# Seven block products in place of eight for the gate and up tiles of a feed-forward layer

## The chip, the cores and the metric

The kernel runs on one core of one Trainium2 chip. The metric is the device time of one execution in microseconds, as the median of several runs. One execution is profiled as well, and its trace is what the rows below come from. TensorE (PE) multiplies, VectorE (DVE) and ScalarE (ACT) do the elementwise work, GpSimd (POOL) helps a little, and SyncE (SP) issues the DMAs that bring the weights in.

## What is computed

The reference is a model of two layers over 544 tokens (512 of a prompt and 32 of a decoding batch), with a model width of 1024. Each layer has a mixer (stick-breaking attention in the first, an RWKV-7 time mix in the second), a cross-attention to a memory, and a feed-forward block. Only the last is touched:

```python
def rms_norm(x, gain):
    xf = x.astype(jnp.float32)
    y = xf * lax.rsqrt(jnp.mean(xf * xf, axis=-1, keepdims=True) + NORM_EPS)
    return (y * gain.astype(jnp.float32)).astype(x.dtype)

def swiglu_ffn(h, w_gate_up, w_down):
    gate, up = jnp.split(h @ w_gate_up, 2, axis=-1)
    return (jax.nn.silu(gate) * up) @ w_down
...
        h = rms_norm(x, p['norm_ffn'][layer])
        x = x + swiglu_ffn(h, p['ffn_w_gate_up'][layer], p['ffn_w_down'][layer])
```

The hidden width is 2816, which is 22 tiles of 128 rows. Everything is float32.

## The kernel before

Activations stand with the model's width on the partitions, so a matrix of weights is cut into units of 1024 x 128, each landing as eight 128 x 128 blocks in one of four slots of `weight_ring`. A float32 product is made of three passes of a faster type (fp32r): every operand is split into a high part, which is the value rounded to that type, and a low part, which is the rest, and PE adds high x high, high x low and low x high in PSUM. The 544 tokens are cut into two halves of 272 (`HALF`), one PSUM bank each. A unit is therefore 8 blocks x 3 passes x 2 halves = 48 matmuls of 128 x 272 (`multiply_unit`, line 235, the matmul on line 259), each with a weight load of its own.

`feed_forward` (line 1945) is one stage with a program for each engine, and it runs once a layer. PE first multiplies the 8 units of the cross-attention's output projection (`o`), then the 44 units of `up` (22 tiles, for each a gate unit and an up unit), then the 24 units of `down`. The up units after the first four run in a loop of 10 passes with two tiles each.

- **DVE** splits each unit in place (`split_unit`, line 277): `take_high` (line 205) writes the high part to one of two buffers, `take_low` (line 210) leaves the low part in the ring. It empties PSUM: `gate` (line 1961) multiplies the gate by the norm's factor, and `multiply` (line 1966) does the same to the up half, multiplies the two, and splits the hidden tile at once into the high and low parts that `down` reads.
- **ACT** does little in this stage: SiLU on each gate tile (line 2045). In the loop a load of its function table stands ahead of every two tiles.
- **SP** loads a unit into a slot as soon as PE is done with the unit in it (`stream_weights`, line 218).

Every engine runs its own instructions strictly in the order written; semaphores tie them together. `down` may start its first unit when 8 hidden tiles have been split, its second with 15, its third with all 22 (`down.ready`). Stages end with a barrier (line 179), and when a stage leaves more than `SEMS_KEPT` semaphores in use they are cleared, with one more barrier (line 173).

Of the kernel before, what the change touches and what calls it, by code (L numbers as in the profile page):

```python
# [23 lines left out]
P = 128  # L24
# [24 lines left out]
SEMS_KEPT = 60  # L49
# [74 lines left out]
class Core:  # L124


    def __init__(self, nc, ctx, ins, outs):
# [5 lines left out]
        self.high, self.high_r = self.aliased("weights_high", [P, 2, UNIT_KT, P])  # L133
        self.psum = ctx.enter_context(nc.psum_tensor("psum", [P, 8, 512], F32))
# [1809 lines left out]

def feed_forward(c, name, o, up, down, nxt, norm, tail, hidden, gated, out, low_rank=None):
# [6 lines left out]
    for job in (up, down) + ((nxt,) if nxt else ()):  # L1952
        job.begin(c)
    silu_taken, multiplied, high, low, scaled = (c.sem(name + x) for x in (
        "_silu_taken", "_multiplied", "_hidden_high", "_hidden_low", "_scaled"))
    down.ready = {0: (low, 8), 1: (low, 15), 2: (low, FT)}
# [4 lines left out]
    def gate(it, i):  # L1961
        nc.vector.wait_ge(*done(c, up, 2 * i, it))
# [3 lines left out]
    def multiply(it, i):  # L1966
        full, tile_high, tile_low = (t[:, bass.ds(it * 2 + i, 1), :] for t in (hidden.full, hidden.high, hidden.low))
        nc.vector.wait_ge(*done(c, up, 2 * i + 1, it))
        nc.vector.tensor_tensor(halves(full), c.psum[:, 4 * i + 2:4 * i + 4, 0:HALF], norm.inverse(),
                                ALU.mult).then_inc(c.slot_emptied[2 * i + 1], 1)  # L1970
        nc.vector.wait_ge(*out_of(c, up, 2 * i + 1, it))
        nc.vector.wait_ge(silu_taken, it * 2 + (i + 1))
        nc.vector.tensor_tensor(full, full, gated[:, i:i + 1, :], ALU.mult).then_inc(multiplied, 1)  # L1973
        nc.vector.wait_ge(multiplied, it * 2 + (i + 1))
        take_high(c, tile_high, full).then_inc(high, 1)
        nc.vector.wait_ge(high, it * 2 + (i + 1))
        take_low(c, tile_low, full, tile_high).then_inc(low, 1)
# [3 lines left out]
    with c.stage() as block:  # L1981
        @block.sync
        def _(sp):
            stream_weights(c, sp, o, up)
            stream_weights(c, sp, up, down)
            if low_rank:
                low_rank.load(sp)
            stream_weights(c, sp, down, nxt)
            if not nxt:
                tail.store(sp, halved)  # L1990

        @block.tensor
        def _(pe):
# [12 lines left out]
            with pe.Fori(1, up.iters) as it:  # L2006
                for u in range(RING):
                    multiply_unit(c, pe, up, it, u)
            if nxt:
                with pe.Fori(0, down.iters) as it:  # L2010
                    for u in range(down.per):
                        multiply_unit(c, pe, down, it, u)
# [7 lines left out]
            else:  # L2020
                for u in range(down.per):
                    multiply_unit(c, pe, down, 0, u)
                    if u >= 3 and u % 3 == 0:
                        tail.turn(pe, u // 3 - 1)
# [11 lines left out]
        @block.scalar  # L2036
        def _(act):
            for k in range(KT):
                norm.scalar(act, k)
            nc.scalar.preload_act_table_set("natural_log_exp_and_others")  # L2040
            norm.take_root(act)
            with act.Fori(0, up.iters) as it:
                for i in range(2):
                    act.wait_ge(*out_of(c, up, 2 * i, it))
                    nc.scalar.activation(gated[:, i, :], gated[:, i, :], ACT.Silu).then_inc(silu_taken, 1)  # L2045
            nc.scalar.preload_act_table_set("natural_log_exp_and_others")
            for k in range(KT):
                tail.scalar(act, k)
                if not nxt and k < KT - 1:
                    tail.keep(act, k)  # L2050
            tail.take_root(act)
            if not nxt:
                tail.divide_by_scalar(act, halved)

        @block.vector
        def _(dve):
# [8 lines left out]
            norm.take_low(dve, KT - 1)  # L2065
            split_unit(c, dve, up, 0, 2)
            dve.wait_ge(norm.inverted, 1)
            gate(0, 0)
            split_unit(c, dve, up, 0, 3)
            multiply(0, 0)  # L2070
            with dve.Fori(1, up.iters) as it:
                split_unit(c, dve, up, it, 0)
                gate(it - 1, 1)
                split_unit(c, dve, up, it, 1)
                multiply(it - 1, 1)
                split_unit(c, dve, up, it, 2)
                gate(it, 0)
                split_unit(c, dve, up, it, 3)
                multiply(it, 0)
            split_unit(c, dve, down, 0, 0)  # L2080
            gate(up.iters - 1, 1)
            split_unit(c, dve, down, 0, 1)
            multiply(up.iters - 1, 1)
            for n in range(down.n):
# [4 lines left out]
                if n + AHEAD < down.n:  # L2089
                    split_unit(c, dve, down, (n + AHEAD) // down.per, (n + AHEAD) % down.per)  # L2090
            if nxt:
# [1251 lines left out]
def build(nc, ins, outs):  # L3343
    with ExitStack() as ctx:
# [27 lines left out]
        def up_job(layer):  # L3372
            w = ins["ffn_w_gate_up"][layer].rearrange("(k p) m -> p k m", p=P)
            return Job(2 * FT, KT, lambda it, u: w[:, :, bass.ds(it * (2 * P) + (u // 2) * P + (u % 2) * FF, P)],
# [124 lines left out]
```

## Time and profile before

| | |
|---|---|
| median of 3 runs | 2107.98 us (2106.9 to 2118.1) |
| the profiled execution | 2109.09 us, of it the span of its instructions 2107.4 us |
| mean granted TensorE clock | 0.986 |
| busy: PE, weight loads, DVE, ACT, POOL | 2007.5, 1886.0, 1144.0, 544.6, 205.2 us |
| instructions | 46663, of them 20636 matmuls |

The two stages of the change stand at about 522 to 983 us (layer 1, counted from one) and at about 1642 to 2107 us (layer 2). A busy share is a mean over stages that have different limits, so it is read by stage. The profile models the end of a matmul, so that matmuls that stream back to back overlap: the spacing of their starts is the rate, the duration is the latency of one.

### The profile page before, as it was taken

How to read it: one execution, taken by the hardware profiler on the slowest of the kernel's cores; microseconds unless marked ns; L12 is line 12 of the kernel's file. 1: busy time of each engine (PE TensorE's matmuls, PEld its weight loads, DVE VectorE, ACT ScalarE, POOL GpSimd, SP SyncE). 2: the span in 40 equal slices, each digit the busy share in tenths (PEclk: the TensorE clock that was granted, in tenths of full speed). 3: DMA queues.
4: the chain of work that ended last, by engine and by line, in shares of the span. 5: the costliest groups of instructions: out<-in, count | busy, mean ns of one | idle time of the engine just before them, and what ended most of it. 6: DMA issues, size and time to landing. Idle time of an engine off the chain costs nothing. (4 is left out here: it accounts for less than half of the span.)

```text
span 2107.4 us, 46663 instructions
## 1 busy us (share of the span) xinstructions
PE 2007.5 (95%) x20636; PEld 1886.0 (89%) x20636; DVE 1144.0 (54%) x1578; ACT 544.6 (26%) x1012; POOL 205.2 (10%) x291
## 2 busy tenths in 40 slices
PE   8998999998999999999999878879999999999998
PEld 7997779996999999997988867668998899999997
DVE  5336886454656555336557734337654565555433
ACT  2005874113210110001237433334212211010111
POOL 5000001000200000110000345410010100000000
PEclk9999999999999999999999999999999999999999
DMA  4234212351323323332222000023351232333222
GB/s 133 82 123 143 61 32 81 121 164 57 90 81 90 90 85 101 95 85 57 70 71 61 8 4 4 4 72 102 103 168 41 61 90 81 88 90 88 83 83 79
DMA packets 299361, 169.77 MB, mean 81 GB/s; under 512 B 10328, under 2 KB 294176, under 8 KB 299200
## 3 DMA queue, kind: packets, MB, share of 16 engines
q1 hardware_dynamic: 294976, 151.25, 25.0%
q10 hardware_dynamic: 4224, 16.12, 2.0%
q8 instruction: 132, 2.16, 0.4%
q14 instruction: 29, 0.24, 0.0%
HBM read 155.94 MB, written 11.41 MB: 79 GB/s over the span
## 5 line engine op out<-in xcount | busy, mean ns | idle before, releaser
L259 PE MATMUL psum<-words_r,weights_high_r 128*128 128x272 f32 (+1 forms) x7808 | 1320.0, 290 | 7.4 <-PEq L179 3.7
L259 PEld LDWEIGHTS psum<-words_r,weights_high_r 128*128 128x128 f32 x7808 | 1117.0, 189 | 19.4 <-issue 15.1
L259 PE MATMUL psum<-words_r,weight_ring_r 128*128 128x272 f32 (+1 forms) x3904 | 829.3, 289 | 0.0
L259 PEld LDWEIGHTS psum<-words_r,weight_ring_r 128*128 128x128 f32 x3904 | 620.2, 190 | 0.0
L205 DVE TENSOR_SCALAR weights_high_r<-weight_ring 128x1024 fp32r<-128x1024 f32 (+1 forms) x258 | 177.9, 690 | 517.2 <-PE psum L259 513.2
L210 DVE TENSOR_TENSOR weight_ring_r<-weight_ring,weights_high_r 128x1024 fp32r<-128x1024 f32 (+1 forms) x264 | 319.4, 1210 | 11.2 <-ACT weights_high_r L350 2.3
L2045 ACT ACTIVATE words<-words 128x544 f32<-128x544 f32 x44 | 29.1, 660 | 448.3 <-DVE words L1963 448.3
L405 POOL TENSOR_TENSOR words<-words,words 128x544 f32<-128x544 f32 x35 | 61.6, 1760 | 766.0 <-ACT words L392 766.0
L2806 PE MATMUL psum<-words 64*64 64x64 f32 (+1 forms) x3168 | 90.8, 236 | 20.7 <-issue 17.5
L2806 PEld LDWEIGHTS psum<-words 64*64 64x64 f32 x3168 | 71.4, 135 | 34.9 <-issue 31.5
L210 DVE TENSOR_TENSOR words_r<-words,words_r 128x544 fp32r<-128x544 f32 (+5 forms) x124 | 87.7, 720 | 7.9 <-ACT words_r L337 2.6
L382 DVE TENSOR_TENSOR words<-psum,words 128x544 f32<-128x544 f32 x40 | 29.0, 725 | 108.1 <-PE psum L259 108.1
L389 ACT ACTIVATE words_r<-words,vector_columns 128x544 fp32r<-128x544 f32 x32 | 24.0, 751 | 154.9 <-DVE words L382 154.9
L392 ACT ACTIVATE words<-words 128x544 f32<-128x544 f32 x40 | 25.8, 646 | 129.9 <-DVE words L382 129.9
L397 DVE SCALAR_TENSOR_TENSOR words_r<-words,vector_columns,words_r 128x544 fp32r<-128x544 f32 x32 | 55.5, 1745 | 0.0
L2680 DVE TENSOR_TENSOR words<-psum,words 128x256 f32<-128x256 f32 x54 | 20.6, 419 | 58.7 <-PE psum L2806 58.7
L1831 POOL TENSOR_TENSOR words<-words,words 128x544 f32<-128x544 f32 x6 | 8.8, 1467 | 375.8 <-ACT words L1817 375.8
L1185 DVE SCALAR_TENSOR_TENSOR words<-psum,words 128x512 f32<-128x512 f32 (+2 forms) x40 | 32.5, 812 | 13.4 <-ACT words L1257 13.0
L928 ACT COPY words<-psum 128x512 f32<-128x512 f32 x16 | 9.4, 588 | 112.0 <-PE psum L867 112.0
L1174 DVE TENSOR_SCALAR words<-psum 128x512 f32<-128x512 f32 (+2 forms) x40 | 32.1, 806 | 5.4 <-PE psum L1057 2.7
L1585 PE MATMUL psum<-words,words 128*128 128x256 f32 x128 | 31.8, 408 | 3.2 <-PEq L179 3.2
L1973 DVE TENSOR_TENSOR words<-words,words 128x544 f32 (+1 forms) x44 | 32.0, 726 | 5.0
(346 smaller groups left out, 1947.7 us busy)
## 6 DMA issues: line engine op xcount, KB each, us to landing
weight_ring<-in_ffn_w_gate_up_dram SPq DMA_DIRECT2D x88, 512.0 KB, 3.9
weight_ring<-in_xa_w_kv_dram SPq DMA_DIRECT2D x32, 512.0 KB, 3.9
weight_ring<-in_ffn_w_down_dram SPq DMA_DIRECT2D x32, 448.0 KB, 3.6
weight_ring<-in_sb_w_qkv_dram SPq DMA_DIRECT2D x24, 512.0 KB, 3.8
weight_ring<-in_xa_w_q_dram SPq DMA_DIRECT2D x16, 512.0 KB, 4.0
weight_ring<-in_xa_w_o_dram SPq DMA_DIRECT2D x16, 512.0 KB, 3.8
weight_ring<-in_ffn_w_down_dram SPq DMA_DIRECT2D x16, 512.0 KB, 3.9
weight_ring<-in_sb_w_o_dram SPq DMA_DIRECT2D x8, 512.0 KB, 3.9
```

The source lines that it names most:

```text
L205: return c.nc.vector.tensor_scalar(high, full, 1.0, None, ALU.mult)
L210: return c.nc.vector.tensor_tensor(low, full, high.bitcast(F32), ALU.subtract)
L259: last = nc.tensor.matmul(c.psum[0:job.m(u), job.bank(q) + h, 0:w], weights[:, k, :], x[:, k, h * w:(h + 1) * w], start=job.opens(u) and k ...
L382: self.c.nc.vector.tensor_tensor(out, psum_of(self.c, self.job, u), out, ALU.add).then_inc(self.c.slot_emptied[self.job.slot(u)], 1)
L397: self.c.nc.vector.scalar_tensor_tensor(out=self.low_part[:, k, :], in0=self.x[:, k, :], scalar=self.gain[:, k:k + 1], in1=self.high_part[ ...
L405: self.c.nc.gpsimd.tensor_tensor(self.total, self.total, self.sq[k % 2], ALU.add).then_inc(self.totalled, 1)
L1174: nc.vector.tensor_scalar(es[p % 2][u], zs[u], EXP_CAP, None, ALU.min).then_inc(capped[u], 1)
L1185: nc.vector.scalar_tensor_tensor(out=sps[u], in0=zs[u], scalar=HD ** -0.5, in1=es[p % 2][u], op0=ALU.mult, op1=ALU.max).then_inc(sp_ready[ ...
L1585: last = mm(scores(g)[:, i, :], q[:, 2 * g + kk, i * P:(i + 1) * P], kv[:, 2 * g + kk, :], start=kk == 0 and i % 2 == 0, stop=kk == 1, ski ...
L1973: nc.vector.tensor_tensor(full, full, gated[:, i:i + 1, :], ALU.mult).then_inc(multiplied, 1)
L2045: nc.scalar.activation(gated[:, i, :], gated[:, i, :], ACT.Silu).then_inc(silu_taken, 1)
L2806: done = mm(dst[to, b, j, :], lhs(h, p, j)[r], rhs(h, p, j)[r], start=start and j == 0, stop=True, skip_group_check=True)
```

## The change

Of the 22 tiles of a layer, the first two stay as they are. For each of the other twenty, the two units (gate and up) and the input are seen as blocks of 2 x 2: `a11`, `a12` are the gate's weights for the first and the last 512 rows of the input, `a21`, `a22` those of up; `b11`, `b21` are the input's rows 0 to 511 and 512 to 1023 for the first 272 tokens, `b12`, `b22` the same for the last 272. Four results are wanted: `c11`, `c12` (the gate for either half of the tokens) and `c21`, `c22` (up). In place of eight products of 12 matmuls (4 blocks x 3 passes), seven are made: `a11`, `a12` and `a22` as they are, and `s1` = a21 + a22, `s3` = a11 - a21, `s2` = s1 - a11, `s4` = a12 - s2; on the input's side `t1` to `t4`, made once a layer. What is added up afterwards goes partly through PSUM (`a11`, `s2`, `s3`, `a22` accumulate in one bank, `s1` and `s4` in another), and partly through three copies that ACT takes of the first bank between products (`snapshot` 0, 1 and 2, after `a11`, `s2` and `s3`).

- PE's order for tile n is a11, s1, s2, a12, s3, then s4 of tile n-1, then a22. All of it is written out, with no loop.
- High parts of the seven weights go from DVE to ACT (`take_high`), low parts stay on DVE, which also makes the four sums of weights.
- The hidden tiles are no longer split as they are made: `hidden_high` (ACT) and `hidden_low` (DVE) follow when the last tile's products are under way, since their place holds the parts of `t1` to `t4` until then.
- In layer 1 the load of the low-rank weights on SP waits for the last product (`low_rank.load`).
- `SEMS_KEPT` goes from 60 to 50; so the semaphores are cleared once more, between layer 2's cross-attention and its feed-forward stage.

The core of the diff:

```diff
-SEMS_KEPT = 60
+SEMS_KEPT = 50
...
+        self.sum_high = ctx.enter_context(nc.sbuf_tensor("sum_high", [P, 3, 4, P], F32R))
...
+class SevenProducts:
+    FIRST = 2
+    X = {"a11": "b11", "a12": "b21", "s4": "b22", "a22": "t4", "s1": "t1", "s2": "t2", "s3": "t3"}
...
+    def bank(self, s, n):
+        if s == "a12":
+            return 4
+        return 2 * (n % 2) + (s in ("s1", "s4"))
...
+    def x_less(self, dve, t, h, other, ready):
+        dve.wait_ge(ready, 4)
+        for k in range(4):
+            self.c.nc.vector.scalar_tensor_tensor(out=self.t_full[t][:, k, :], in0=self.x[:, 4 + k, h * HALF:(h + 1) * HALF],
...
+    def take_high(self, act, s, n):
+        if s in ("a11", "a12"):
+            act.wait_ge(*self.landed(n, 0))
+        elif s == "a22":
+            act.wait_ge(*self.landed(n, 1))
+        else:
+            act.wait_ge(self.summed[s], n - self.FIRST + 1)
+        if n > self.FIRST:
+            act.wait_ge(*self.done(s, n - 1))
...
+        self.c.nc.scalar.activation(self.highs[s], self.words(s, n), ACT.Copy).then_inc(self.high_taken[s], 1)
...
+    def multiply(self, pe, s, n):
+        pe.wait_ge(self.low_taken[s], k + 1)
...
+        if s == "s2":
+            pe.wait_ge(self.snapped[0], k + 1)
...
+        if s == "s3":
+            pe.wait_ge(self.snapped[1], k + 1)
+        if s == "a22":
+            pe.wait_ge(self.snapped[2], k + 1)
+        if s == "s4":
+            pe.wait_ge(self.added["c22"], k + 1)
...
+        for j in range(4):
+            for i, (w, v) in enumerate(((high, x_high), (high, x_low), (low, x_high))):
+                last = nc.tensor.matmul(self.psum(s, n), w[:, j, :], v[:, j, :], start=opens and j == 0 and i == 0,
+                                        stop=j == 3 and i == 2, skip_group_check=True)
...
+    def snapshot(self, act, i, n):
+        s, reader = (("a11", "c11"), ("s2", "c12"), ("s3", "c22"))[i]
+        act.wait_ge(*self.done(s, n))
...
+    def hidden_high(act, n):
+        act.wait_ge(multiplied, n + 1)
+        act.wait_ge(*seven.done(("s1", "s2", "s3", "a22", "s4", "s4")[n // 4], last_tile))
+        nc.scalar.activation(hidden.high[:, n, :], hidden.full[:, n, :], ACT.Copy).then_inc(high, 1)
...
             if low_rank:
+                sp.wait_ge(*seven.done("s4", last_tile))
                 low_rank.load(sp)
...
-            with pe.Fori(1, up.iters) as it:
-                for u in range(RING):
-                    multiply_unit(c, pe, up, it, u)
+            for n in range(first, FT):
+                for s in ("a11", "s1", "s2", "a12", "s3"):
+                    seven.multiply(pe, s, n)
+                if n > first:
+                    seven.multiply(pe, "s4", n - 1)
+                seven.multiply(pe, "a22", n)
+            seven.multiply(pe, "s4", last_tile)
...
+            for n in range(first, FT):
+                seven.snapshot(act, 0, n)
+                if n - 2 >= first:
+                    silu(act, n - 2)
+                seven.take_high(act, "a22", n)
+                seven.snapshot(act, 1, n)
+                seven.take_high(act, "s4", n)
+                if n < last_tile:
+                    seven.take_high(act, "a11", n + 1)
+                else:
+                    for j in range(4):
+                        hidden_high(act, j)
+                seven.snapshot(act, 2, n)
+                if n < last_tile:
+                    for s in ("s1", "s2", "a12", "s3"):
+                        seven.take_high(act, s, n + 1)
...
+            for n in range(first, last_tile):
+                seven.sum(dve, "s1", n + 1)
+                seven.sum(dve, "s3", n + 1)
+                seven.sum(dve, "s2", n + 1)
+                seven.take_low(dve, "a22", n)
+                seven.gate_half(dve, "c11", n)
+                seven.take_low(dve, "s4", n)
+                seven.take_low(dve, "a11", n + 1)
+                seven.up_second(dve, n)
+                seven.take_low(dve, "s1", n + 1)
...
+                seven.sum(dve, "s4", n + 1)
...
+                seven.take_low(dve, "s2", n + 1)
+                seven.up_first(dve, n)
+                seven.take_low(dve, "a12", n + 1)
+                seven.scale_up_second(dve, n)
+                seven.take_low(dve, "s3", n + 1)
...
+            for j in range(4):
+                hidden_low(dve, j)
+            seven.up_second(dve, last_tile)
             split_unit(c, dve, down, 0, 0)
...
```

How the instructions stand on ACT, for one pass of the loop before (two tiles; SiLU reads and writes `words_1088_84`, the gate tiles):

```order
L2045 ACT_TABLE_LOAD
L2045 ACTIVATE words_1088_84<-words_1088_84 128x544 [waits slot_emptied0]
L2044 REGISTER_ALU
L2045 ACTIVATE words_1088_84<-words_1088_84 128x544 [waits slot_emptied2]
L2042 REGISTER_ALU
```

And now, for one tile in the middle (L2136 is a snapshot from PSUM, L2084 a high part: `sum_high` is that of s4, s1 or s2, `weights_high_r` that of a weight as it is; a semaphore is printed under the first name that its number had, so `suffix_taken_2` is the sum of s4):

```order
L2136 ACTIVATE words_272_6093<-psum 128x272 [waits xa0_c11_added_5,xa0_a11_multiplied_5]
L2215 ACTIVATE words_1088_84<-words_1088_84 128x544 [waits xa0_gate_scaled_5]
L2084 ACTIVATE weights_high_r<-weight_ring 128x512 [waits unit_done3,weights_landed1]
L2136 ACTIVATE words_272_6095<-psum 128x272 [waits xa0_c12_added_5,xa0_s2_multiplied_5]
L2084 ACTIVATE sum_high<-words_512_10131 128x512 [waits xa0_s4_multiplied_5,suffix_taken_2]
L2084 ACTIVATE weights_high_r<-weight_ring 128x512 [waits xa0_a11_multiplied_5,weights_landed2]
L2136 ACTIVATE words_272_6097<-psum 128x272 [waits xa0_c22_added_5,xa0_s3_multiplied_5]
L2084 ACTIVATE sum_high<-words_512_10110 128x512 [waits xa0_s1_multiplied_5,weights_ready_y1_2]
L2084 ACTIVATE sum_high<-words_512_10113 128x512 [waits xa0_s2_multiplied_5,weights_ready_s_2]
```

ACT has gone from one instruction a tile to eleven, and its high part of s4 (fifth row) stands, with a wait for the product s4 of the tile before, two rows ahead of the third snapshot (seventh row).

On PE, where s4 of the tile before ends and a22 begins, the rows are these (`words_512_r` is the low part of s4; the last row of the first product is its twelfth matmul):

```order
L2126 MATMUL psum<-words_4352_r,sum_high 128x272 [waits xa0_c22_added_5,xa0_s4_low_5]
L2126 MATMUL psum<-words_4352_r,sum_high 128x272
...
L2126 MATMUL psum<-words_4352_r,sum_high 128x272 x2
L2126 MATMUL psum<-words_4352_r,words_512_r 128x272
L2126 MATMUL psum<-words_1088_r,weights_high_r 128x272 [waits xa0_snapped2_5,xa0_a22_low_5]
L2126 MATMUL psum<-words_1088_r,weights_high_r 128x272
```

Before, PE's waits within the loop were for a unit's split and for an emptied bank; now each product waits for its low part, and a22, which follows s4 of the tile before with nothing between, also for the third snapshot.

## Rows read from the trace of the kernel before

**Rows 1.** The page, busy time of each engine over the span.
```profile
PE 2007.5 (95%) x20636; PEld 1886.0 (89%) x20636; DVE 1144.0 (54%) x1578; ACT 544.6 (26%) x1012; POOL 205.2 (10%) x291
```
**Rows 2.** Busy by stretch (us, PE, PEld, DVE, ACT, POOL, clock, DMA): one tile, then layer 1's tiles.
```profile
599.48:611.50 12.02, 12.02 (x98) 12.02 (x98) 7.01 (x9) 0.66 (x1) 0.00 (x0) 1.00 0.30 89
575.00:840.00 265.00, 265.00 (x2114) 264.84 (x2114) 153.90 (x199) 31.30 (x36) 0.00 (x0) 1.00 0.31 88
```
**Rows 3.** Timeline of PE (start, us, what), memory projection: three matmuls a block, one bank.
```profile
427.31 0.40 PE L259 MATMUL psum<-words_r,weights_high_r 128*128 128x256 f32 x2
...
427.67 0.40 PE L259 MATMUL psum<-words_r,weights_high_r 128*128 128x256 f32 x2
```
**Rows 4.** Groups of ACT's instructions by shape (count, busy us, mean ns).
```profile
L1262 ACT ACTIVATE words_r<-words 128x512 fp32r<-128x512 f32 x16 | 10.1, 630 | 0.0
L1748 ACT ACTIVATE words_r<-psum 128x512 fp32r<-128x512 f32 x16 | 9.6, 601 | 19.9 <-PE psum L1619 19.9
L2731 ACT COPY words<-psum 128x256 f32<-128x256 f32 x18 | 6.4, 373 | 14.7 <-DVE words L2646 14.7
```
**Rows 5.** Timeline of ACT, a 512-column instruction and the next.
```profile
207.66 0.63 ACT L1257 ACTIVATE words<-words 128x512 f32<-128x512 f32 x1
208.20 0.85 ACT L1267 ACTIVATE words<-psum 128x832 f32<-128x832 f32 x1
```
**Rows 6.** Timeline where ACT releases PE, and where PE releases ACT.
```profile
509.44 0.58 ACT L1742 COPY words<-psum 128x512 f32<-128x512 f32 x1
...
510.17 3.67 PE L1619 MATMUL psum<-words,words 128*128 128x512 f32 x8 [0.53 <-ACT words L1742]
...
513.90 1.04 PE L1603 MATMUL psum<-ident,words 128*128 128x128 f32 x8
...
514.97 0.59 ACT L1742 COPY words<-psum 128x512 f32<-128x512 f32 x1 [0.16 <-PE psum L1603]
```
**Rows 7.** The page, one matmul's latency: the costliest group.
```profile
L259 PE MATMUL psum<-words_r,weights_high_r 128*128 128x272 f32 (+1 forms) x7808 | 1320.0, 290 | 7.4 <-PEq L179 3.7
```
**Rows 8.** Groups of DVE's instructions by shape (count, busy us, mean ns).
```profile
L1973 DVE TENSOR_TENSOR words<-words,words 128x544 f32 (+1 forms) x44 | 32.0, 726 | 5.0
L2680 DVE TENSOR_TENSOR words<-psum,words 128x256 f32<-128x256 f32 x54 | 20.6, 419 | 58.7 <-PE psum L2806 58.7
L2113 DVE SCALAR_TENSOR_TENSOR words<-words,vector_columns,words 128x544 f32<-128x544 f32 x24 | 18.3, 780 | 1.6 <-PE psum L2189 1.6
L210 DVE TENSOR_TENSOR words_r<-words,words_r 128x512 fp32r<-128x512 f32 x16 | 11.0, 687 | 0.7
```
**Rows 9.** Timeline of DVE in that tile, a unit's split and what follows.
```profile
601.45 0.69 DVE L205 TENSOR_SCALAR weights_high_r<-weight_ring 128x1024 fp32r<-128x1024 f32 x1 [1.24 <-PE psum L259]
602.17 1.22 DVE L210 TENSOR_TENSOR weight_ring_r<-weight_ring,weights_high_r 128x1024 fp32r<-128x1024 f32 x1
603.32 0.72 DVE L1963 TENSOR_TENSOR words<-psum,words 128x544 f32<-128x544 f32 x1
```
**Rows 10.** The page, the gate and up loads: count, KB, median us to landing.
```profile
weight_ring<-in_ffn_w_gate_up_dram SPq DMA_DIRECT2D x88, 512.0 KB, 3.9
```
**Rows 11.** Groups of PE's instructions: one that followed a clearing of semaphores.
```profile
L325 PE MATMUL psum<-ones,ident 128*128 128x128 f32 x78 | 9.6, 276 | 1.7 <-PEq L173 1.7
```
**Rows 12.** Timeline of PE where it resumes after a wait (us in brackets).
```profile
15.84 1.24 PE L259 MATMUL psum<-words_r,weights_high_r 128*128 128x272 f32 x4 [3.19 <-DVE words_r L784]
...
521.78 0.74 PE L259 MATMUL psum<-words_r,weights_high_r 128*128 128x272 f32 x4 [1.83 <-PEq L179]
...
1642.30 0.75 PE L259 MATMUL psum<-words_r,weights_high_r 128*128 128x272 f32 x4 [1.83 <-PEq L179]
```
**Rows 13.** Busy by stretch, behind the first of those waits, later, and behind the other two.
```profile
15.80:18.80 3.00, 2.96 (x13) 2.99 (x14) 3.00 (x5) 2.89 (x6) 0.00 (x0) 0.50 0.71 175
19.00:22.00 3.00, 3.00 (x26) 3.00 (x25) 2.96 (x5) 0.00 (x0) 3.00 (x3) 1.00 0.02 5
...
521.78:525.20 3.42, 3.42 (x27) 3.42 (x28) 0.00 (x0) 0.00 (x0) 0.00 (x0) 1.00 0.02 5
...
1642.30:1645.70 3.40, 3.40 (x20) 3.40 (x21) 0.00 (x0) 0.00 (x0) 0.00 (x0) 0.69 0.03 5
```

More of the change, by code:

```diff
@@ L1970, in multiply @@
                                 ALU.mult).then_inc(c.slot_emptied[2 * i + 1], 1)
[L1971 to L1977, printed above, removed]
+    def multiply(dve, n):
+        if n < first:
+            dve.wait_ge(*out_of(c, up, 2 * n + 1))
+        else:
+            dve.wait_ge(seven.added["c21"], n - first + 1)
+            dve.wait_ge(seven.up_scaled, n - first + 1)
+        dve.wait_ge(silu_taken, n + 1)
+        full = hidden.full[:, n, :]
+        nc.vector.tensor_tensor(full, full, gated[:, n % 2, :], ALU.mult).then_inc(multiplied, 1)
@@ L1979, in feed_forward, with hidden_low @@
+    def hidden_low(dve, n):
+        dve.wait_ge(high, n + 1)
+        take_low(c, hidden.low[:, n, :], hidden.full[:, n, :], hidden.high[:, n, :]).then_inc(low, 1)
     halved = c.sem(name + "_halved")
@@ L2020, in _ @@
             else:
[L2021 to L2024, printed above, removed]
                 tail.sum_total(pe)
@@ L2040, in _ @@
             nc.scalar.preload_act_table_set("natural_log_exp_and_others")
+            seven.scale_b12(act)
+            seven.scale_t1(act)
             norm.take_root(act)
[L2042 to L2045, printed above, removed]
+            silu(act, 0)
+            for t in ("t1", "t2", "t3", "t4"):
+                seven.take_t_high(act, t)
+            for s in ("a11", "s1", "s2", "a12"):
+                seven.take_high(act, s, first)
+            silu(act, 1)
+            seven.take_high(act, "s3", first)
+            for n in range(first, FT):
[7 more added lines that the diff above has]
+                    seven.take_high(act, "a11", n + 1)
+                else:
+                    for j in range(4):
[4 more added lines that the diff above has]
+                        seven.take_high(act, s, n + 1)
+            for j in range(4, 8):
+                hidden_high(act, j)
+            silu(act, FT - 2)
+            for j in range(8, 16):
+                hidden_high(act, j)
+            silu(act, FT - 1)
+            for j in range(16, FT):
+                hidden_high(act, j)
             nc.scalar.preload_act_table_set("natural_log_exp_and_others")
@@ new lines, in _ @@
+            seven.take_t_low(dve, "t2")
+            for s in ("s1", "s3", "s2", "s4"):
+                seven.sum(dve, s, first)
+            seven.take_t_low(dve, "t3")
+            gate(1)
+            seven.take_low(dve, "a11", first)
+            seven.take_low(dve, "s1", first)
+            seven.take_low(dve, "s2", first)
+            seven.take_low(dve, "a12", first)
+            seven.take_t_low(dve, "t4")
+            scale_up(1)
+            seven.take_low(dve, "s3", first)
+            multiply(dve, 1)
@@ new lines, in _ @@
+            seven.take_low(dve, "a22", last_tile)
+            seven.gate_half(dve, "c11", last_tile)
+            seven.take_low(dve, "s4", last_tile)
+            for j in range(4):
+                hidden_low(dve, j)
+            seven.up_second(dve, last_tile)
+            split_unit(c, dve, down, 0, 0)
+            seven.gate_half(dve, "c12", last_tile - 1)
+            seven.scale_gate(dve, last_tile - 1)
+            for j in range(4, 8):
+                hidden_low(dve, j)
+            seven.up_first(dve, last_tile)
@@ L2084, in _ @@
+            seven.scale_up_second(dve, last_tile)
+            multiply(dve, last_tile - 1)
+            split_unit(c, dve, down, 0, 1)
+            seven.gate_half(dve, "c12", last_tile)
+            seven.scale_gate(dve, last_tile)
+            for j in range(8, 16):
+                hidden_low(dve, j)
+            multiply(dve, last_tile)
             for n in range(down.n):
@@ L2090, in _ @@
                     split_unit(c, dve, down, (n + AHEAD) // down.per, (n + AHEAD) % down.per)
+                if n == 0:
+                    for j in range(16, FT):
+                        hidden_low(dve, j)
             if nxt:
```

214 lines of the change are left out of this document (190 added, 24 removed).

## The prediction

> **What bounds the kernel now.** I read the page's busy shares first, then the busy times of the stretch that the change touches, then the timelines of the engines that gain work. PE is busy 95% of the span, ACT 26% and DVE 54% [rows 1]; but these are means over unlike stages. Within the touched stage PE has no gap at all: one tile takes 12.02 us and PE is busy for all of it, and so for the whole 265 us around it [rows 2]. DVE works 7.0 us of that tile and ACT 0.7 us. So the stage is bound by PE's stream of matmuls, 96 a tile, and 12.02 / 96 = 0.125 us is the spacing of their starts. A matmul removed there is worth 0.125 us, as long as nothing makes PE wait.
>
> **What the change removes.** Seven products of 12 matmuls are 84, so 12 fewer: 12 x 0.125 = 1.50 us a tile, 30.0 us for the 20 tiles of a layer. The twelve matmuls of a product fill one bank in a row, where before two banks took turns. The memory's projection already does that, with 256 columns, at three matmuls in 0.36 us [rows 3], so 0.120 each; I keep 0.125 for 272 columns (bounds 0.120 and 0.128, 8 us at the upper one over both layers). The order of the program shows the 84 matmuls, so the change does what it says. The loads stay 88 of 512 KB [rows 10], and ACT's repeated table loads in the loop go, which cost nothing, since ACT idles.
>
> **What it adds in each tile.** By volume it all fits. On DVE there are now 11 instructions of 512 columns at 0.61 us (0.687 [rows 8], less the 0.08 by which the next one overlaps [rows 9]), five of 272 at 0.36 (between 0.419 for 256 columns and 0.687 for 512, less 0.08) and two of 544 at 0.65: 9.8 us, against 84 x 0.125 = 10.5 us on PE. ACT has seven high parts at 0.54 us [rows 5], three snapshots and a SiLU, some 5.3 us. What decides is the order.
>
> PE goes from s4 of the tile before straight to a22, and a22 waits for the third snapshot. On ACT that snapshot stands behind two high parts, and the first of these, that of s4, may not overwrite its buffer until PE is done with s4 of the tile before. So nothing of this chain can start before s4 ends, and PE has nothing to do until the chain has ended. Counted from the start of s4's last matmul: its latency 0.29 [rows 7]; ACT starts about 0.05 later (0.03 in the row where PE releases ACT [rows 6]; there is one more wait here); the high part of s4 0.54; that of the next a11 0.54 (630 ns long [rows 4], 0.54 from start to start [rows 5]); the snapshot 0.39 (272 columns from PSUM, between 373 ns for 256 and 601 for 512 [rows 4]); PE resumes 0.15 after ACT's end (509.44 + 0.58 to 510.17 [rows 6]). That is 1.96 us, and without the wait the next matmul would start at 0.125: **PE stands still for 1.83 us in each tile** (bounds 1.6 and 2.0, from shorter and longer wake-ups). It is more than the 1.50 us saved. It applies to tiles 3 to 20, 18 a layer: 33.0 us.
>
> What this cover hides: DVE takes the low part of s4 and then that of the next a11, which PE needs one product later; 0.29 + 0.05 + 0.63 + 0.03 + 0.61 + 0.69 + 0.15 = 2.45 us after the same start, while PE comes there at 0.125 + 1.83 + 1.50 = 3.46. If ACT's wait went away, this one would hold PE for 2.45 - 1.63 = 0.8 us instead. The load of a slot that a22 frees lands 3.9 us later [rows 10], DVE adds sums and a low part (some 2.6 us), and PE asks for the result after 9.0 us, so the loads stay hidden.
>
> **What it adds at both ends, each layer.**
> - *Start.* From the split of the fourth unit on, DVE works without a break up to a11's low part: that split 1.87 [rows 9], three of 544 columns 1.95, the twelve scaled differences of `x_less` at 0.415 (780 ns for 544 columns, less 0.285 for half the columns, less 0.08 [rows 8]) 5.0, three low parts of 1088 columns 3.6, four sums 2.6, the low part 0.7: 15.7 us. PE's two units meanwhile last 12.0. With the wake-ups PE waits 3.9 us.
> - *First tile.* No s4 lies ahead of its a22, and the snapshot alone costs 0.29 + 0.05 + 0.39 + 0.15 - 0.125 = 0.75 us.
> - *Last tile.* Four `hidden_high` of 544 columns (0.57 each) stand where a high part stood: 1.83 + 1.74 = 3.6 us.
> - *Down.* The hidden tiles are split here now. From the third snapshot until down's third unit may start, DVE has five instructions of 272 columns (1.8), 22 of 544 (14.3), three units' splits (5.2, two of them shorter) and some 0.5 of waits for itself: 21.8 us. PE has 12 + 12 + 48 + 42 = 114 matmuls in that time, 14.3 us. PE waits 7.5 us, in three pieces of about 3.6, 2.5 and 1.4.
>
> Elsewhere the same work stood in the loop under PE's cover, so there is nothing to take off for it. The four terms are 15.8 us, bounds 12 and 19.
>
> **Two smaller terms.** The additional clearing of semaphores makes PE wait: 1.7 us in the row of another [rows 11], taken as 1.5 (bounds 0 and 2). And the clock: behind a wait of 3.19 us [rows 12] the granted clock stood at 0.50 (1.2 of 2.4 GHz), and PE started 13 matmuls in 3.0 us where it later starts 26 [rows 13], so 13 x 0.125 = 1.6 us are lost. Waits of that size are new at the start and in the last tile; those before down are covered by DVE. Four times 1.6 would be 6.4; I take 3, because a lowered stretch can lie partly in the wait (bounds 0 and 7).
>
> **Sum.** Each layer: -30.0 + 33.0 + 3.9 + 0.75 + 3.6 + 7.5 = +18.7; both 37.5; with 1.5 and 3, +42 us on the profiled execution's 2109.1: 2151. That execution lies 1.1 us above the median, so the forecast is **2150 us**. Its own range is 2134 to 2167, from 36 x 0.2 for the wait, 6 for the ends, and the smaller terms.
>
> **The rivals.**
> - *The clock falls in every tile.* PE now rests about 1.7 us in each. The trace has two waits of 1.83 us ahead of the same matmuls: after one the clock stayed at 1.00, after the other it was 0.69 over the next 3.4 us [rows 12, 13]. Either way is open, then. If half of the 36 waits are followed by a loss of 1.6 us, that is 29 us more: 2179. The Trainium skill, in TensorE: Matmul & The Clock Gate, section HAM oscillation — how this bites in real kernels, describes a kernel in which bursts of matmuls parted by waits are throttled anew behind each wait. By that rule, all 36 would pay: 58 us, 2208. The trace agrees for one of its two waits. Chance 0.25.
> - *Only the next wait is left.* If the third snapshot came in time after all, a11's low part would hold PE for 0.8 us: 18 x 0.8 = 14.4 stand in place of 33.0 and 1.8 in place of 3.6: -30.0 + 14.4 + 3.9 + 0.75 + 1.8 + 7.5 = -1.6 a layer, and with the two smaller terms 2110. Against it speaks the order on ACT. Chance 0.07.
> - *Faster.* The wait between s4 and a22 decides, 19 times a layer with the last tile's. The rest of the ends is 3.9 + 0.75 + 1.74 + 7.5 = 13.9 us and the smaller terms 2.2 a layer, so below (30.0 - 13.9 - 2.2) / 19 = 0.73 us a wait the saved matmuls would show; with none at all each layer gives back 14 us: 2081. For it speak the volumes, which fit everywhere; against it, that the latency, one copy, the snapshot and the wake-ups alone make 1.3 us. Chance 0.06.
>
> **How the numbers follow.** My case has 0.62, the rivals 0.25, 0.07 and 0.06. 0.5%, some 10.5 us, is about what a measurement of this kernel can tell from no change. Faster by more is the last rival alone, 0.06; within it the one before, with a bit of my own lower end, 0.08; slower has the rest, 0.86. The range that holds the time 8 times in 10 reaches from 2128, under my case's lower end, to 2188, over the clock's case with half of the waits.
>
> **What would show it.** The page of the changed kernel: PE's busy share in the stage falls from all to about 85%, its idle time before the group of the seven products' matmuls is some 80 to 100 us, and most of it ends with ACT's snapshot (in the waits' view PE waits for ACT 36 times, about 1.8 us each, and once a layer 3.6). A tile takes 12.3 to 12.4 us. ACT's high part of s4 starts right behind s4's last matmul. I am wrong if PE's waits within the tile are under 1 us or end with DVE or a DMA; if the granted clock over the tiles is below 0.97, the first rival is right; if the time is off while the tile takes 12.35 us, the ends are.

## The result, and the profile after

The changed kernel takes **2153.6 us** (median of four runs, 2150.9 to 2158.9) against 2110.0 for the kernel before (median of four runs, 2106.9 to 2118.1): a ratio of 1.020, 95% interval 1.017 to 1.024. Forecast were 2150 with a range of 2128 to 2188. The profiled execution took 2151.3 us, 42.2 more than that of before.

Row of the page that answers to [rows 1] (busy us, share of the span, instructions), and two of its groups (line, engine, operation, count, busy us, mean ns, idle time before them and who ended it):

```profile
PE 1967.5 (92%) x20156; PEld 1839.4 (86%) x20156; DVE 1303.8 (61%) x2008; ACT 748.2 (35%) x1460; POOL 205.8 (10%) x291
...
L2126 PE MATMUL psum<-words_r,weights_high_r 128*128 128x272 f32 x1280 | 251.2, 293 | 75.8 <-ACT words L2136 68.1
...
L2084 ACT ACTIVATE sum_high<-words 128x512 fp32r<-128x512 f32 x120 | 71.0, 624 | 163.1 <-PE psum L2126 158.9
```

PE has 480 matmuls fewer, as meant, and 40 us less work; but it stands still for 75.8 us ahead of the seven products (line 2126 is `multiply`, 2136 the snapshot, 2084 `take_high`), and 68.1 of that end with ACT. The waits' view (who waited for whom, us in total, times, longest) says how often:

```profile
PE psum L2126 <- ACT words L2136: 68.1, 40, 3.3
...
PE psum L2126 <- DVE weight_ring_r L211: 7.8, 2, 3.9
PE psum L260 <- DVE words_r L211: 6.4, 4, 2.4
```

40 waits for the snapshot are the 36 in tiles 3 to 20, and one in the first and one in the last tile of each layer; the second row is the start of the twenty tiles, the third is most of down. Busy times by stretch answer to [rows 2]: one tile, and eighteen of layer 1 (columns as there).

```profile
629.80:642.27 12.47, 10.80 (x86) 10.61 (x85) 9.82 (x18) 5.37 (x11) 0.00 (x0) 1.00 0.29 84
618.00:842.00 224.00, 194.25 (x1512) 190.87 (x1512) 174.97 (x321) 96.49 (x198) 0.00 (x0) 1.00 0.29 85
```

A tile takes 12.47 us (from the start of one a22 to that of the next) in place of 12.02, PE works 87% of it, and the granted clock is 1.00, which is 2.4 GHz, throughout. Within the tile this is the place where the time goes (timeline: start us, duration us, engine; in brackets the idle time before and its releaser). PE ends s4 of the tile before; then ACT's chain runs, with DVE's low part of s4 beside it, and PE stands still:

```profile
629.79 0.29 PE L2126 MATMUL psum<-words_r,words_r 128*128 128x272 f32 x1
630.18 0.63 ACT L2084 ACTIVATE sum_high<-words 128x512 fp32r<-128x512 f32 x1 [4.17 <-PE psum L2126]
630.72 0.61 ACT L2084 ACTIVATE weights_high_r<-weight_ring 128x512 fp32r<-128x512 f32 x1
630.84 0.69 DVE L211 TENSOR_TENSOR words_r<-words,sum_high 128x512 fp32r<-128x512 f32 x1 [2.53 <-ACT sum_high L2084]
631.23 0.38 ACT L2136 ACTIVATE words<-psum 128x272 f32<-128x272 f32 x1
...
631.76 0.49 PE L2126 MATMUL psum<-words_r,weights_high_r 128*128 128x272 f32 x2 [1.67 <-ACT words L2136]
```

From the start of s4's last matmul to that of a22's first are 1.96 us, where 0.125 would do: 1.84 lost. It is the chain of the prediction link by link: latency 0.29, wake-up 0.10, high part of s4 0.54, of a11 0.51, snapshot 0.38, wake-up 0.14. ACT had idled for 4.17 us ahead of it, and what ended that was PE's s4, which gives the one buffer free.

**Where the 42 us lie**, by the starts of PE's matmuls in both profiled executions (both layers):

| part | forecast | measured |
|---|---|---|
| 480 matmuls fewer (what is left starts 0.1254 apart on average) | -60.0 | -58.7 |
| 36 waits in the tiles: 1.96 - 0.125 each | +66.0 | +66.1 |
| the second matmul behind a wait, 0.20 in place of 0.125, 36 times | 0 | +2.8 |
| start of the twenty tiles, 2 x 4.04 | +7.8 | +8.1 |
| first tile, 2 x 0.74 | +1.5 | +1.5 |
| last tile, 2 x 3.50 | +7.2 | +7.0 |
| down: waits 9.4, half clock around them 7.2, restarts 1.1 | +15.0 | +17.7 |
| half clock at the start | +3.0 | +3.2 |
| one clearing of semaphores more: 3.93 - 2.42 | +1.5 | +1.5 |
| code outside the two layers, the same in both | 0 | -7.0 |

The code of the last row is the same in all the kernels here, and their profiled executions still take anything between 1194 and 1206 us outside the two layers (1204 for before, 1198 for the change), so this row can't be put down to the change. It also means that the sum came out closer than its terms: the two layers and the clearing became 49 us longer, 7 more than the 42 of the forecast, and the code outside took 7 less, for which the forecast had no term. So a part of some us is better read from **the two layers alone**, in each from the start of o's first matmul to that of the last matmul which closes the stage behind down (in layer 1 the last of the twenty of `keep_clock`, in layer 2 the kernel's last): 903.4 us before, 951.0 after, both layers together.

### The profile page after: what moved, and what is told of

It reads as the page before. It is cut to its first block and busy times, and to the rows that moved or that the text cites. A ratio compares the mean times of both kernels' runs of the same rounds, so it can differ in the third digit from the quotient of the medians.

```text
span 2149.4 us, 46995 instructions
## 1 busy us (share of the span) xinstructions
PE 1967.5 (92%) x20156; PEld 1839.4 (86%) x20156; DVE 1303.8 (61%) x2008; ACT 748.2 (35%) x1460; POOL 205.8 (10%) x291
## 5 line engine op out<-in xcount | busy, mean ns | idle before, releaser
L260 PE MATMUL psum<-words_r,weights_high_r 128*128 128x272 f32 (+1 forms) x5248 | 899.5, 292 | 17.5 <-DVE words_r L211 6.4
L260 PEld LDWEIGHTS psum<-words_r,weights_high_r 128*128 128x128 f32 x5248 | 757.6, 190 | 30.4 <-issue 26.3
L260 PE MATMUL psum<-words_r,weight_ring_r 128*128 128x272 f32 (+1 forms) x2624 | 565.9, 289 | 0.0
L211 DVE TENSOR_TENSOR weight_ring_r<-weight_ring,weights_high_r 128x512 fp32r<-128x512 f32 (+2 forms) x344 | 330.7, 961 | 7.3 <-ACT weights_high_r L351 1.2
L2126 PE MATMUL psum<-words_r,weights_high_r 128*128 128x272 f32 x1280 | 251.2, 293 | 75.8 <-ACT words L2136 68.1
L2126 PEld LDWEIGHTS psum<-words_r,weights_high_r 128*128 128x128 f32 x1280 | 204.0, 191 | 84.0 <-issue 75.9
L2126 PE MATMUL psum<-words_r,weight_ring_r 128*128 128x272 f32 x640 | 187.8, 293 | 0.0
L2126 PE MATMUL psum<-words_r,sum_high 128*128 128x272 f32 x960 | 185.8, 290 | 0.0
L2126 PEld LDWEIGHTS psum<-words_r,sum_high 128*128 128x128 f32 x960 | 152.9, 191 | 0.0
L2126 PE MATMUL psum<-words_r,words_r 128*128 128x272 f32 x480 | 139.2, 290 | 0.0
L2084 ACT ACTIVATE sum_high<-words 128x512 fp32r<-128x512 f32 x120 | 71.0, 624 | 163.1 <-PE psum L2126 158.9
L3150 PE MATMUL psum<-words 64*64 64x64 f32 (+1 forms) x3168 | 89.8, 237 | 17.7 <-issue 14.6
L2084 ACT ACTIVATE weights_high_r<-weight_ring 128x512 fp32r<-128x512 f32 x160 | 95.2, 619 | 0.0
```

What stands on the lines that cost most here:

```text
L211: return c.nc.vector.tensor_tensor(low, full, high.bitcast(F32), ALU.subtract)
L260: last = nc.tensor.matmul(c.psum[0:job.m(u), job.bank(q) + h, 0:w], weights[:, k, :], x[:, k, h * w:(h + 1) * w], start=job.opens(u) and k ...
L2084: self.c.nc.scalar.activation(self.highs[s], self.words(s, n), ACT.Copy).then_inc(self.high_taken[s], 1)
L2126: last = nc.tensor.matmul(self.psum(s, n), w[:, j, :], v[:, j, :], start=opens and j == 0 and i == 0, stop=j == 3 and i == 2, skip_group_c ...
L3150: done = mm(dst[to, b, j, :], lhs(h, p, j)[r], rhs(h, p, j)[r], start=start and j == 0, stop=True, skip_group_check=True)
```

## The experiments

The theory: PE's wait in a tile is ACT's chain behind the end of s4, which can't begin earlier since s4's high part has one buffer. The main rival: DVE has 9.8 of 12.5 us to do in a tile and would hold PE whatever ACT does. Of each edit the core is shown, with `...` for the rest.

**The third snapshot ahead of both high parts** (on ACT, in `feed_forward`):

```
+                seven.snapshot(act, 2, n)
                 seven.take_high(act, "s4", n)
...
-                seven.snapshot(act, 2, n)
```

> ACT takes the third snapshot before the high part of s4 instead of two high parts later; nothing else is changed, and the single buffer for s4's high part stays. Theory (PE's 1.84 us in a tile are ACT's chain behind the end of s4): the wait before a22 goes, and the next thing that is late holds PE one product later, DVE's low part of the next a11, by the forecast's 0.8 us. 36 x (1.84 - 0.8) = 37 us less; in the last tile up to 3.3 us a layer go too, but down may take them back. From 2153.6: 2110 to 2120, and PE's waits within the tiles end with DVE. Rival (DVE has no time left in a tile, and PE would stand as long wherever the snapshot is taken): within 5 us of 2153.6.

Measured 2123.9 us (2114.0 to 2129.3), above the 2110 to 2120 expected; two layers 918.7, 32 less, where at least 37 were expected. A tile takes 11.53 us in place of 12.47. The waits now are

```profile
PE psum L2126 <- DVE weight_ring_r L211: 29.5, 38, 3.9
PE psum L260 <- DVE words_r L211: 11.1, 5, 4.0
PE psum L2126 <- DVE words L2157: 6.0, 2, 3.0
```

Between the last matmul of a22 and the first of a11 are 0.89 us in each of the 36 tiles, so 0.77 lost, forecast 0.8: what is late next is what the prediction named. The third row is what I had overlooked: in the last tile s4 waits for `up_second` (line 2157), which stands on DVE behind four low parts of hidden tiles, so that wait stayed 3 us; and more matmuls ran at 1.2 GHz behind the waits at the ends (some 180 in the two layers, 120 in the change, at 0.1 us more each).

**Two buffers for s4's high part**; the second lies in words of the norm's sum that are free by then.

```
+        self.s4_high = [c.sum_high[:, 2], c.flat(9, w, at=3 * T, dtype=F32R).rearrange("p (k n) -> p k n", k=4)]
...
-        if n > self.FIRST:
-            act.wait_ge(*self.done(s, n - 1))
+        if s == "s4":
+            if n > self.FIRST + 1:
+                act.wait_ge(*self.done(s, n - 2))
+        elif n > self.FIRST:
+            act.wait_ge(*self.done(s, n - 1))
```

> A second buffer for s4's high part (the tiles take turns), in words that are free in this stage; ACT then waits for the s4 of two tiles before, which is long done. The order on every engine stays. Theory: both the 1.84 us before a22 and the 0.08 by which the first matmul behind a wait is late go from 36 tiles (36 x 1.91 = 69 us), and a11's low part is not late either; of the last tile's 3.5 us a layer down's first wait may take back all. From 2153.6: 2077 to 2087, PE without a wait in tiles 3 to 20, a tile at 84 x 0.125 = 10.5 us. Rival 1 (what comes next in line, a11's low part, still holds PE by 0.8 us): 69 - 29 = 40 less, 2114. Rival 2 (DVE, 9.8 of 10.5 us by count, can't keep up, since its instructions wait for one another): above 2114, with PE's waits ending with DVE.

Measured **2080.7 us** (2079.9 to 2085.6), ratio to before 0.987 (0.984 to 0.989): the same products, now faster than before. Layers 875.4. Busy times by stretch, tiles 3 to 20 of layer 1:

```profile
612.00:802.00 190.00, 189.44 (x1507) 189.47 (x1508) 177.83 (x323) 96.87 (x199) 0.00 (x0) 1.00 0.35 102
```

PE has no wait left in them, a tile takes 10.56 us (by the starts of its matmuls, 84 x 0.1257), and DVE is busy 94% of it without holding PE. Both rivals fall: DVE does keep up, and a11's low part is not late, since s4's no longer stands late ahead of it. The last tile's 3.5 us went too; down's first wait, 4.06 us now, took 1.6 to 1.7 of them back in each layer.

**The chain made longer** by one unused copy on ACT, behind the wait for s4 and ahead of its high part.

```
...
+            self.c.nc.scalar.activation(self.c.flat(9, 4 * P, at=3 * T), self.norm.inv[:, 0:4 * P], ACT.Copy).then_inc(self.spent, 1)
         self.c.nc.scalar.activation(self.highs[s], self.words(s, n), ACT.Copy).then_inc(self.high_taken[s], 1)
```

> A copy of 512 columns more on ACT, of words that are not used, between the wait for s4 of the tile before and the high part of s4, in tiles 4 to 22: the chain that PE waits for is longer by one such copy, 0.53 us. Theory: every wait in a tile is 2.37 us in place of 1.84: 36 x 0.53 = 19 us, with the last tiles' 20: 2174. Rival on the clock: in the changed kernel the half clock followed each of PE's waits from 2.2 us up (first layer) and none of the 36 of 1.84; if the longer wait brings it in every tile, at the 1.5 us that each of those cost, 36 x 1.5 = 54 more: 2228. Rival (ACT is not what PE waits for): 2154.

Measured 2197.4 us (2193.0 to 2203.5), layers 995.6, between theory and rival. Each of the 36 gaps grew from 1.96 to 2.47 us: 0.51 x 36 = 18, as the theory has it. But behind **16 of the 36** the clock stood at 1.2 GHz for 12 to 16 matmuls; such a tile took 14.4 to 14.5 us in place of 12.98, some 1.5 us more: 23 in all. Two of these gaps and what follows them, by stretch (the clock is the third value from the right):

```profile
656.70:659.20 2.50, 0.37 (x3) 0.15 (x2) 0.86 (x2) 2.04 (x5) 0.00 (x0) 1.00 0.19 55
659.20:662.70 3.50, 3.45 (x16) 3.48 (x17) 3.50 (x8) 1.99 (x4) 0.00 (x0) 0.54 0.00 0
671.20:673.80 2.60, 0.42 (x5) 0.22 (x3) 0.95 (x2) 2.13 (x5) 0.00 (x0) 1.00 0.17 49
673.80:677.30 3.50, 3.50 (x28) 3.50 (x29) 3.50 (x8) 2.14 (x5) 0.00 (x0) 1.00 0.12 35
```

The same wait, 16 matmuls in 3.5 us behind the one and 28 behind the other. The 16 are mostly every second tile: of the 14 steps from one lowered tile to the next within a layer, ten are of two tiles, three of three, one of one. Why just these, no run here shows. So the prediction's first rival is a mechanism of this kernel, half a microsecond of waiting away.

**s4 of the tile before ahead of s3** on PE, one buffer, ACT as it was.

```
-                for s in ("a11", "s1", "s2", "a12", "s3"):
+                for s in ("a11", "s1", "s2", "a12"):
                     seven.multiply(pe, s, n)
                 if n > first:
                     seven.multiply(pe, "s4", n - 1)
+                seven.multiply(pe, "s3", n)
                 seven.multiply(pe, "a22", n)
```

> PE takes s4 of the tile before ahead of s3 and not behind it; one buffer, ACT's order as it was. Theory: ACT's two high parts, 0.34 + 0.54 + 0.54 us behind the start of s4's last matmul, now fall under the 1.5 us of s3, and a22 waits only for the snapshot of s3 that PE has just ended: 0.75 us as in the first tile (0.74 there). 36 x (1.84 - 0.75) = 39 us less, and the last tile's wait falls from 3.5 to about 2.1: 2110 to 2117, a tile at 11.3 us. Rival (DVE has no time left): within 5 us of 2153.6.

Measured 2112.4 us (2109.2 to 2117.1), ratio to before 1.001 (0.9995 to 1.003), layers 909.2. The gap before a22 is 0.87 us in tiles 3 to 20, 0.74 lost; PE still waits for ACT 40 times, but for 25.6 us in place of 68.1:

```profile
PE psum L2126 <- ACT words L2136: 25.6, 40, 1.8
```

Three ways to take ACT's two copies out from between s4 and the snapshot, with DVE's work as it was, gave what the chain says: the theory stands.

**The ends**, all on top of the two buffers. First GpSimd, which has next to nothing to do in this stage, was given work of DVE's: at the start (t3's difference, the low parts of t3 and t4, the rest in the order in which PE asks for it), and ahead of down (nine of the 22 `hidden_low`).

```
+            seven.t3_less_b12(pool)
+            for t in ("t3", "t4"):
+                seven.take_t_low_pooled(pool, t)
```

> On top of the two buffers for s4 (2080.65), the work ahead of the first of the twenty tiles in another order: DVE takes what PE asks for first first, three pieces of DVE's go to engines that idle there (the scaling for t3 to ACT, t3's difference and the low parts of t3 and t4 to GpSimd), and two products of the first two tiles come later. Theory (PE's start wait of 4.04 us a layer, and the 1.5 us of half clock behind it, are DVE's work that PE's two units don't cover): both go in both layers, 11 us: 2070, the first wait of the stage being the 0.74 of the first tile. Rival 1 (DVE is so full that the work that was put off holds PE a tile later): 2078 to 2081. Rival 2 (GpSimd, at 1.76 us for a copy-like instruction of 544 columns, comes too late with 1088, or slows DVE beside it): PE waits at s3 or a22 of the first tile, over 2076.

```
+    POOLED = {0: (3, 5, 7), 1: (10, 12, 14), 2: (17, 19, 21)}
...
+            for n in pooled:
+                hidden_low_pooled(pool, n)
```

> On top of the two buffers for s4 (2080.65), GpSimd takes nine of the 22 low parts of the hidden tiles that DVE takes ahead of down. Theory (PE's waits at down, 6.5 us in the first layer and 6.2 in the second, are DVE's 27 us without a break): 9 x 0.64 = 5.8 us a layer leave DVE, some 4 to 5 of it shows on PE, and half of the half clock behind these waits, 1.5 us each, goes too: 2067 to 2073. Rival (GpSimd, nine times 1.76 = 15.8 us, or ACT's 22 high parts, is what comes last then): 2075 to 2081, and PE waits for GpSimd.

> Two buffers for s4, the new order at the start and GpSimd's nine low parts ahead of down together. If the two ends add up: 11 and 10 us below 2080.65, 2056 to 2064. If GpSimd slows DVE wherever both work, or the one end takes back what the other gives: above 2068.

Measured 2076.4 us (2071.1 to 2080.1), **2094.7** (2094.2 to 2096.6) and 2092.0 (2088.1 to 2095.0); layers 875.0, 887.1 and 884.3 against 875.4. The start gained nothing in the layers of its profiled execution (the slowest of its four runs; the median is 4 us lower), and at down the help cost 12 us. Not because GpSimd was late: PE's waits ahead of down grew, and they still end with DVE, none with GpSimd (first the run with the two buffers alone, then the one with help at down):

```profile
PE psum L260 <- DVE words_r L211: 12.0, 5, 3.8
...
PE psum L260 <- DVE words_r L211: 19.8, 6, 4.5
```

It was DVE that became slow. In the run with work at the start, DVE's sums beside GpSimd's two low parts (timeline):

```profile
586.40 0.68 DVE L2071 TENSOR_TENSOR words<-weight_ring 128x512 f32<-128x512 f32 x1
587.19 2.86 DVE L2075 TENSOR_TENSOR weight_ring<-weight_ring 128x512 f32<-128x512 f32 x1
589.97 3.00 DVE L2079 TENSOR_TENSOR words<-words,weight_ring 128x512 f32<-128x512 f32 x1
593.07 0.69 DVE L211 TENSOR_TENSOR weight_ring_r<-weight_ring,weights_high_r 128x512 fp32r<-128x512 f32 x1
...
586.87 5.55 POOL L2054 TENSOR_TENSOR words_r<-words,words_r 128x1088 fp32r<-128x1088 f32 x2 [5.69 <-ACT words_r L2050]
```

Two sums take 2.86 and 3.00 us in place of 0.69, and the instruction of the same size after GpSimd's end 0.69 again. At down it is the same, but not for the instruction that reads PSUM:

```profile
814.23 0.43 DVE L2164 TENSOR_TENSOR words<-psum,words 128x272 f32<-128x272 f32 x1
814.58 1.49 DVE L206 TENSOR_SCALAR weights_high_r<-weight_ring 128x1024 fp32r<-128x1024 f32 x1
816.11 2.25 DVE L211 TENSOR_TENSOR weight_ring_r<-weight_ring,weights_high_r 128x1024 fp32r<-128x1024 f32 x1
...
811.87 5.40 POOL L2240 TENSOR_TENSOR words_r<-words,words_r 128x544 fp32r<-128x544 f32 x3 [234.75 <-ACT words_r L2230]
```

Alone the latter two take 0.68 and 1.23. The Trainium skill says it: GPSIMD Engine Reference, section 1. Specifications, has GpSimd share its SBUF interfaces with VectorE, in contention with VectorE's two-port modes and with instructions of two SBUF inputs. The trace agrees, and adds the price.

The rows show more than a slower pace: DVE's instruction ends shortly after the GpSimd instruction beside it. GpSimd's two low parts at the start end at 589.50 and 592.42, DVE's two sums at 590.05 and 592.98; the last one at down ends at 817.27, DVE's at 818.36, and the copy before it ends 0.55 us after GpSimd's second. So beside GpSimd, DVE does one such instruction in the time of each of GpSimd's, however short its own is.

**The start without GpSimd** (its order differs from that of the run above in a few places more), and then the high parts of down's first two units on ACT:

```
+            seven.t3_less_b12(dve)
...
+            seven.take_low(dve, "a11", first)
+            seven.take_t_low(dve, "t1")
+            seven.take_low(dve, "s1", first)
+            seven.x_less(dve, "t4", 0, seven.t_full["t2"], seven.t_ready["t2"])
```

> Two buffers for s4 and the new order at the start without GpSimd: ACT scales for t3, DVE takes everything else itself, and three of its 544-column pieces come up to two tiles later. Theory (it was GpSimd beside DVE that took back the gain of the order at the start): DVE's instructions keep their lengths, 0.69 us for 512 columns; the start wait of 4.04 us a layer and its half clock give way to waits under 0.7 each, 1.5 us in all, 2.5 to 4 us a layer less: 2072 to 2076 from 2080.65, and DVE's low parts ahead of a11 are through before PE's fourth unit ends. Rival (the order itself can't gain, DVE being full, whoever helps): 2078 to 2083.

```
-            split_unit(c, dve, down, 0, 0)
+            down_low(dve, 0)
...
+            down_high(act, 0)
             for j in range(4, 8):
                 hidden_high(act, j)
```

> As the run with the new order and without GpSimd, and the high parts of down's first two units (0.69 and 0.62 us of DVE) go to ACT, which has pauses of 1.7 to 4.0 us there. Theory (PE's waits at down are DVE's unbroken work): 1.3 us a layer less, 2 to 3 us in all against the run without it. Rival (ACT's in-order queue then holds up the hidden tiles' high parts): no gain or a loss.

Measured **2071.6 us** (2068.3 to 2080.0), ratio to before 0.982 (0.980 to 0.984), layers 867.9; and 2071.9 (2063.0 to 2074.9), layers 865.6. Both ran on another chip than the experiments above, so they are compared through the kernel before and the layers. The order at the start is worth 7.6 us of the layers: the wait of 4.04 us and the half clock behind it gave way to three of 0.4 to 0.65. DVE's sums there have their usual length:

```profile
583.78 0.69 DVE L2067 TENSOR_TENSOR words<-weight_ring 128x512 f32<-128x512 f32 x1
584.57 0.69 DVE L2071 TENSOR_TENSOR weight_ring<-weight_ring 128x512 f32<-128x512 f32 x1
585.18 0.68 DVE L2075 TENSOR_TENSOR words<-words,weight_ring 128x512 f32<-128x512 f32 x1
```

The move to ACT saves 2.3 us in the layers, as expected, but the two medians can't tell it from nothing; it stays unproven. Either is some 40 us faster than the kernel before, 2112.1 beside them.

## Why the prediction was right

**The verdict and the time**: slower, 2150 against 2153.6; that near a time was luck in part, as the table shows. What carried it, the wait between s4 and a22, was right in its place, its cause and its size (1.83 forecast, 1.84 measured): it was computed as a chain of single durations and not from busy shares, which left ACT idle for more than half of the tile. That the saved 30 us a layer are real the second run shows: without the wait a tile takes 10.56 us in place of 12.02, 29 us less over twenty tiles.

**The links** were not all right. The wake-up of ACT took 0.10 and not 0.05, the second copy, the snapshot and PE's wake-up together 0.05 less; they cancelled. The signs promised are there but for two sizes: the tile takes 12.47 us and not 12.3 to 12.4, since the second matmul behind each wait is late as well, and PE's idle time on the page is 75.8 and not 80 to 100 us, since it counts a wait from the end of the matmul before, 1.67 us of the 1.84. One bound was worked out wrongly and used nowhere else: 0.128 in place of 0.125 us for 3360 matmuls makes 10 us, not 8.

**What would be late next**, a11's low part by 0.8 us, was right as long as s4's low part comes late (0.77 in the first run); the text had it hold PE "if ACT's wait went away", and with the second buffer it did not, because then s4's low part is early as well.

**The ends.** Start, first and last tile are within 0.3 us. Down I had put at 7.5 us a layer of pure waiting; PE waited 4.8 and 4.6. The term was right as time and wrong in kind: in layer 2 DVE worked from PE's a22 to the third unit, 21.8 of 22.1 us:

```profile
1989.05:2011.17 22.12, 18.03 (x114) 17.47 (x115) 21.81 (x36) 12.42 (x21) 0.00 (x0) 0.85 0.16 46
```

21.8 is what the working had for DVE; 114 matmuls at 0.125 are 14.25, and the other 7.9 are 4.6 of waits and 3.3 of half clock and restarts. Where DVE sets the end, as here, PE at 1.2 GHz only fills a wait. So the clock term of 3 was enough, though half clock took 9.8 us more of the layers than before: all four waits that the term was meant for brought it, 3.2 us at the start and 2.9 behind the last tiles' waits, but the 2.9 (in the table a part of down's 7.2) lie in time that DVE needed anyway (in layer 1 it is busy 16.8 of the 17.1 us from a22 to the third unit). In layer 1 the sum is 1.8 higher: two GpSimd instructions for another stage ran there from 857.83 to 860.51, and DVE's eight low parts took 6.86 us in place of 5.17 in layer 2:

```profile
856.13 6.86 DVE L211 TENSOR_TENSOR words_r<-words,words_r 128x544 fp32r<-128x544 f32 x8
```

**The rivals.** *The clock in every tile*: it fell in none of the 36, at 0.5 us more in 16 of 36. By the rule of the Trainium skill that the prediction had cited (TensorE: Matmul & The Clock Gate, section HAM oscillation — how this bites in real kernels) every burst behind a wait is throttled anew; the trace does not agree at the change's wait, and agrees in part at the longer one. The kernel that this section describes waits about 3 to 5 us each time, longer than either, so the 2208 took its rule further than it is stated. The chance of 0.25 was not too high for how near the half clock was. *Only the next wait* is what the first experiment made of the kernel, 2124, above the 2110 worked out for it: the last tile's wait did not shrink, and some 60 matmuls more ran at half clock, 6 us. *Faster* needed a wait under 0.73 us; at 0.74 (s4 ahead of s3) the kernel takes as long as before, at none 2080.7 (forecast for that case 2081).

## What to carry to other kernels

Before work is taken from the engine that bounds a stage, walk once along what its next instruction needs, engine by engine, from the last thing that frees the first buffer: here one 2 KB buffer a partition decided between 2% slower and 1.3% faster, though every engine's work fitted both times. Where two products follow each other on PE, nothing that starts with the end of the first should stand in front of what the second waits for on an in-order queue. And an idle GpSimd was no help here to a full DVE that works from SBUF: in the rows above, each instruction given to it held up one of DVE's.

## What was not expected of the hardware

- DVE's instructions that read only SBUF take about two to four times as long beside GpSimd (0.69 to 2.86 and 3.00 us for a sum of 512 columns, 0.68 to 1.49 for a one-input copy of 1024, 1.23 to 2.25 for a two-input one), because they end only 0.5 to 1.1 us after the GpSimd instruction beside them; those that read PSUM take 0.43 us either way. GpSimd's own, of 544 columns, took 1.86 us on average there, against 1.76 for its other group of that size in the same run (line 406).
- A wait of the same length, 2.47 us from start to start, is followed by 1.2 GHz in 16 cases and by 2.4 GHz in 20; waits of 1.96 us were followed by 2.4 GHz in all 36. Each lowered stretch cost 1.4 to 1.5 us, and most of them stood two tiles apart.
- The second matmul behind a wait starts 0.20 us after the first and not 0.125, at full clock too: 2.8 us over the 36 waits.
